# First modulation of a diffusion backbone: another order of loads and pieces, and twelve filler products behind each quarter of the second tile

## What is computed

```python
mod = jax.nn.silu(c) @ w_mod[l] + b_mod[l]                 # c for latents, c_ctx for context tokens
shift, scale, gate = jnp.split(mod, 3, axis=-1)
xn = rmsnorm(x, norm_w) * (1.0 + scale[:, None, :]) + shift[:, None, :]
proj = xn @ w_in
aq, ak, av, ag, ch, cb, cc, cg, gq, gk, gv, gg, glr = jnp.split(proj, SPLIT_POINTS, axis=-1)
...
x = x + gate[:, None, :] * mix
```

## Time and profile before

| | |
|---|---|
| median of 3 runs | 2151.84 us (2149.92 to 2151.88) |
| profiled execution | 2152.64 us, span 2150.8 us, granted clock 0.997 |
| TensorE busy | 2106.6 us, 98% of the span |
| VectorE busy | 1442.9 us, 67% |
| ScalarE busy | 647.9 us, 30% |
| first modulation | about 24 us (first quarter) to 128 us (last flip) |

### The profile page before, as it was taken

One profiled execution on the slowest core, in us unless ns is written; L12 is line 12 of the kernel. 1 busy time (PEld: TensorE's weight loads), 2 busy tenths in 40 slices (PEclk: granted clock), 3 DMA queues, 4 the chain that ended last, 5 costly groups with the idle time before them and its releaser, 6 DMA issues.

```text
span 2150.8 us, 35018 instructions
## 1 busy us (share of the span) xinstructions
PE 2106.6 (98%) x13815; PEld 1895.5 (88%) x13815; DVE 1442.9 (67%) x2797; ACT 647.9 (30%) x1092; POOL 194.0 (9%) x125
## 2 busy tenths in 40 slices
PE   5999999999999999999999999999999999999998
PEld 3778887887999999999998888888899999999998
DVE  5869888999665656766366355466666566676644
ACT  4232221321333334442134212232133333343302
POOL 0000000000000000523221000000000000043331
PEclk9999999999999999999999999999999999999999
DMA  9989786774333324564435546445343233366443
GB/s 351 376 293 320 230 282 230 234 245 160 117 105 101 99 77 135 187 210 144 121 120 162 170 149 203 132 139 150 120 129 104 75 97 105 90 209 208 152 123 141
DMA packets 357333, 365.42 MB, mean 170 GB/s; under 512 B 17670, under 2 KB 264156, under 8 KB 356572
## 3 DMA queue, kind: packets, MB, share of 16 engines
q1 hardware_dynamic: 328528, 320.67, 46.6%
q10 hardware_dynamic: 28684, 43.09, 5.3%
HBM read 304.98 MB, written 58.72 MB: 169 GB/s over the span
## 4 chain that ended last, share of the span: by engine, by line
PE 70%; DVE 2%; issue 1%; ACT 1%; DMA 1%; SPq 0%; ACTq 0%; DVEq 0%
PE psP L921 20%; PE psP L865 16%; PE psP L942 10%; PE psO L1148 6%; PE psT L875 4%; PE psT L1148 3%; PE psO L1121 3%; PE psP L1076 3%; PE psT L1087 2%; PE psP L1160 0%; PE psP L1238 0%; DVE xf L2025 0%; PE psP L1246 0%; PE psP L834 0%; DMA old<-x_scratch 0%
## 5 line engine op out<-in xcount | busy, mean ns | idle before, releaser
L1831 DVE SCALAR_TENSOR_TENSOR macc<-mraw,cond,macc 128x384 f32<-128x384 f32 (+1 forms) x960 | 389.2, 477 | 0.0
L865 PE MATMUL psP<-x_high,high 128*128 128x512 f32 x864 | 342.3, 396 | 0.6 <-DVE x_low L1887 0.6
L865 PE MATMUL psP<-x_high,low 128*128 128x512 f32 x864 | 336.6, 390 | 0.0
L865 PE MATMUL psP<-x_low,high 128*128 128x512 f32 x864 | 336.4, 389 | 0.0
L1336 ACT ACTIVATE high<-raw 128x1024 fp32r<-128x1024 f32 x128 | 135.4, 1059 | 594.3 <-PE psT L875 493.3
L921 PE MATMUL psP<-x_high,high 128*128 128x320 f32 x1024 | 242.6, 318 | 0.0
L921 PE MATMUL psP<-x_high,low 128*128 128x320 f32 x1024 | 233.4, 309 | 0.0
L921 PE MATMUL psP<-x_low,high 128*128 128x320 f32 x1024 | 232.9, 309 | 0.0
L1849 DVE TENSOR_TENSOR low<-raw,high 128x1024 fp32r<-128x1024 f32 x128 | 163.3, 1277 | 64.8 <-ACT high L1336 64.7
L865 PEld LDWEIGHTS psP<-x_high,high 128*128 128x128 f32 x864 | 162.1, 188 | 41.6 <-issue 7.7
L865 PEld LDWEIGHTS psP<-x_high,low 128*128 128x128 f32 x864 | 162.2, 188 | 34.5
(11 more groups left out here) (327 smaller groups left out, 3715.5 us busy)
## 6 DMA issues: line engine op xcount, KB each, us to landing
raw<-in_w_in_dram SPq DMA_DIRECT2D x132, 512.0 KB, 6.0
wmod<-in_w_mod_dram SPq DMA_DIRECT2D x32, 1024.0 KB, 8.2
mraw<-in_w_mod_dram SPq DMA_DIRECT2D x64, 512.0 KB, 4.5
mraw<-in_w_mod_dram SPq DMA_DIRECT2D x32, 1024.0 KB, 7.3
raw<-in_w_in_dram SPq DMA_DIRECT2D x32, 1024.0 KB, 5.7
raw<-in_w_out_dram SPq DMA_DIRECT2D x64, 512.0 KB, 4.2
old<-x_scratch SPq DMA_DIRECT2D x64, 320.0 KB, 3.2
xf<-proj_scratch SPq DMA_DIRECT2D x48, 320.0 KB, 3.6
```

Of the source, the lines that this page charges most:

```text
L865: mm = pe.matmul(latent_ps[m], own, moved, start=(k == 0 and w is whole and x is x_high), stop=(k == KT - 1 and w is rest))
L1831: m = dve.scalar_tensor_tensor(acc[:, v, 0:width], mraw[hf][:, k, 0:width], c, acc[:, v, 0:width], ALU.mult, ALU.add)
```

## The change

It moves work within the first modulation and adds fillers. Loads: tile 1's quarters go out ahead of chunk 0; in later blocks chunk 2j goes out behind quarters 0 and 1 of the odd tile instead of ahead of it. TensorE: tile 0's quarters stand behind columns 3, 6, 8 and 11 of the input instead of 3, 7, 11 and 15; tile 1's quarters stand behind the wait for the whole of x, each followed by `keep_busy(12)` on the bank `psP[0]`; two pieces of block 0 come ahead of tile 2, and 0, 1, 1, 1 and 1, 2, 1, 2 behind the quarters of tiles 2 and 3. ScalarE: block 0 casts chunk 1 in the middle of its columns. VectorE: the low part of chunk 2j stands behind the modulation's sums instead of ahead of the early sums.

```diff
+FIRST_QUARTERS = (3, 6, 8, 11)
+PIECES_LEAD, PIECES_FIRST = 2, [0, 1, 1, 1, 1, 2, 1, 2]
...
-            for t in range(MOD_CHUNKS):
-                mod_block(t)
-                front_chunk(0, t)
-                if t % 2 == 1:
-                    extra_tiles(t // 2)
+            for j in range(BLOCKS):
+                mod_block(2 * j, range(4))
+                if j == 0:
+                    mod_block(2 * j + 1, range(4))
+                    front_chunk(0, BLOCK_C * j)
+                else:
+                    mod_block(2 * j + 1, range(SUMMED_Q))
+                    front_chunk(0, BLOCK_C * j)
+                    mod_block(2 * j + 1, range(SUMMED_Q, 4))
+                front_chunk(0, BLOCK_C * j + 1)
+                extra_tiles(j)
...
-                if k % 4 == 3:
-                    mod_quarter(0, k // 4)
+                if k in FIRST_QUARTERS:
+                    mod_quarter(0, FIRST_QUARTERS.index(k))
...
-            for q in range(4):
-                mod_quarter(1, q)
...
-            def keep_busy(count):
+            def keep_busy(count, bank=psT):
 
                 for _ in range(count):
-                    pe.matmul(psT[:, 0:P], ident[:], ident[:], start=True, stop=True)
+                    pe.matmul(bank[:, 0:P], ident[:], ident[:], start=True, stop=True)
...
                     pe.wait_ge(s["x_taken"], KT)
+                    for q in range(4):
+                        mod_quarter(1, q)
+                        keep_busy(12, psP[0])
                     piece = 0
+                    for _ in range(PIECES_LEAD):
+                        block_piece(piece)
+                        piece += 1
                     for t in range(2, MOD_CHUNKS):
                         for q in range(4):
                             mod_quarter(t, q)
-                            for _ in range(PIECES_AFTER[t % 2 * 4 + q]):
+                            for _ in range((PIECES_FIRST if t < 4 else PIECES_AFTER)[t % 2 * 4 + q]):
                                 block_piece(piece)
                                 piece += 1
...
-                        for n in (2 * j, 2 * j + 1):
-                            cast_chunk(n)
+                        cast_chunk(BLOCK_C * j)
+                        if j > 0:
+                            cast_chunk(BLOCK_C * j + 1)
                         act.wait_ge(s["mod_ready"], j + 1)
                         for k in range(j * BLOCK_K, (j + 1) * BLOCK_K):
+                            if k == BLOCK_K // 2:
+                                cast_chunk(BLOCK_C * j + 1)
...
                         if j > 0:
                             flip(2 * j)
-                        chunk_low(BLOCK_C * j)
-                        if j > 0:
                             early_sums(2 * j + 1)
                         flip(2 * j + 1)
...
                                 2 * j + 2, j * BLOCK_K, BLOCK_K)
+                        chunk_low(BLOCK_C * j)
                         for k in range(j * BLOCK_K, (j + 1) * BLOCK_K):
```

More of the change, by code:

```diff
@@ L97 @@
 PIECES_AFTER, PIECES_LAST = [0, 2, 1, 2, 1, 2, 1, 2], 3
+FIRST_QUARTERS = (3, 6, 8, 11)
+PIECES_LEAD, PIECES_FIRST = 2, [0, 1, 1, 1, 1, 2, 1, 2]
 assert sum(PIECES_AFTER) + PIECES_LAST == BLOCK_PIECES and len(PIECES_AFTER) == 8
+assert PIECES_LEAD + sum(PIECES_FIRST) + PIECES_LAST == BLOCK_PIECES and len(PIECES_FIRST) == 8
 EXTRA_SLOT = RING - 1
@@ L477, in _, with mod_block @@
             wm = io["w_mod"][0].rearrange("(k p) n -> p k n", p=P)
-            def mod_block(t):
-                for q in range(4):
+            def mod_block(t, quarters):
+                for q in quarters:
                     sp.wait_ge(s[f"wmod_used{q}"], t + SEED)
```

## The result

The changed kernel takes 2156.37 us (median of 9 runs, 2155.14 to 2157.92), the kernel before 2151.88 us in the same measurement (9 runs, 2149.92 to 2154.03). The ratio is 1.002, with a 95% interval of 1.0011 to 1.0029: 4.5 us more, where 3.2 were forecast. The profiled execution took 2157.92 us, with a span of 2156.1 us.

What follows compares the result with a forecast made beforehand. TensorE bounds the kernel, so the first modulation's end shifts everything behind it. Flip 1 +7.6, flip 2 +6.9, flip 3 +5.4, then 1.1 us gained twice: +3.2 us, 2155.0 us (range 2151.3 to 2158.8).

Steps and rivals of the forecast that it cites:

- Part 1: Earlier tile 0 quarters, new load order: tile 1 starts 0.6 us later, at 40.1, and waits for no load.
- Part 2: Fillers behind tile 1's quarters: 2.68 us a group, three on the path, flip 1 7.6 us late; clock worth 0.5.
- Part 3: Two pieces ahead of tile 2: fill former load time, give back 0.7 us; flip 2 at 66.6, 6.9 us late.
- Part 4: Early sums ahead of the low part, blocks 1 to 3: gains 1.1 us each, 1.5 in block 1; loads in time.
- rival (a): Loads of odd tiles' third and fourth quarters become the bound, slower: 2157.2 to 2159.8 us; chance 0.18.
- The sum: Flip 7 comes 3.2 us later, TensorE has no gap behind it: 2155.0 us against the median, 0.15% more.
- (b): Loads in tiles 1 and 2 cover the fillers, only the gains are left: -3.7 us, 2148.1; chance 0.06.
- (c): Part 4 brings nothing, but another engine behind 128 us absorbs the delay: about 2151.8 us; chance 0.09.

Runs made afterwards that it cites:

- the loads back: Chunk 2j's load again behind all four quarters of the odd tile, on the changed kernel without fillers (0.9977), with the last group only (0.9991), with all fillers (1.0026).
- six fillers: Changed kernel with 6 instead of 12 fillers behind each quarter of tile 1: 2153.74 us, ratio 1.0001.
- the fillers alone: Kernel before plus only 12 fillers behind each quarter of tile 1, behind the wait for the whole of x: 2158.58 us, ratio 1.0027.

## Why the prediction was right, and where it wasn't

**Part 1.** Right in what matters: the loads of tile 1 cover nothing, as no quarter of it waited for one. The start was wrong by 0.6 us: the fourth stall is there, but the first one was 0.86 us instead of 1.45, and so tile 1 starts at 39.48 as before. I had taken the stalls of before as fixed.

**Part 2.** Right in mechanism and nearly in size: a group took 2.87 us instead of 2.68 (40.47 to 43.34), so three groups 0.6 us more. By luck this error made up for that of the start: flip 1 came at 52.19, forecast 52.2. The fillers' worth was put at 0.5 us, from the two slow quarters. It is 1.5 us in this order, as the pieces now stand where the clock is low (the kernel without fillers shows it). The row about the quarters was the wrong one to price it: I should have asked what runs there after the change. The sign is not touched.

**Part 3.** Right: the first piece's second half at 56.93 (57.15 forecast), tile 2 at 59.19 (59.4), flip 2 at 66.33 (66.6).

**Part 4.** Right for VectorE's order, which was also shown by itself: the even-to-odd stretch is 11.18 us in blocks 2 and 3, 1.14 us less, and flip 3 came 11.19 us behind flip 2. In block 1 the load of tile 3's third quarter, forecast to land at 72.0 and be read at 72.2, landed at 73.3. The step that failed is the time from issue to landing: I took the loads one behind the other at full rate. The four quarters' loads that were issued between 58 and 70 us took 8.0 us in the median (9.1 us in the second trace), against 5.4 and 6.9 us in the earlier trace rows. In the first trace this hid behind the early sums. In the second the load came 1.1 us later still, and the clock fell with it. That is rival (a)'s place, in block 1 only, and with another price than the one I gave: 1.1 us of load and 1.5 us of low clock, together 2.6 us from flip 2 to flip 3. In blocks 2 and 3 no trace has such a wait.

**The sum.** Flip 7 was forecast 3.2 us later and came 2.7 us later in one trace and 4.9 in the other (4.4 against the second trace of before). The measured 4.5 us, with its interval of 2.4 to 6.2 us, holds the forecast. That it lies so near is in part luck, as behind 500 us single executions moved by 1 to 3 us, which the sum had at nothing. Rivals (b) and (c) are out: without the fillers the kernel is 9.7 us quicker by the ratios, and the shift of flip 7 isn't absorbed in the projection. That the rest moves along with flip 7, as TensorE has no gap behind it, held until 500 us. Behind that I had overlooked stretches of small products in which the clock can fall (1.4 to 1.5 us between the layers, or nothing) and drifts of about a us in either direction.

**The two halves.** By flip 7, the new order without fillers gives 3.7 us and the fillers take 6.4 (8.7 by the second trace of the changed kernel). By the ratios, it is 5.4 us (0.25%) and 9.7 us (0.45%). The fillers were the whole loss, and without them the change is a gain: 0.9975 (0.9964 to 0.9986).

**What stays open.** Whether a kernel's own timing decides how often the clock falls between the layers. All four traces with the loads back have the fall, two of the ten others have it, and the three kernels of those four differ in their fillers; no run tested why. The kernel with one group and the loads back has the earliest flip 7 and falls there in both its traces, with a further 2.3 and 3.0 us lost behind 1400 us; by its ratio it gains 1.9 us, where flip 7 says 6.4. The one with all fillers and the loads back is also worse by its ratio than by its flips. It also stays open why one group behind the last quarter costs 3.1 us in the medians. One or two traces of each kernel can't settle these.

## What to carry over

Ahead of a filler stands the question who waits for the next instruction on that engine. Fillers between the quarters of a critical tile cost their full time three times, less what the clock that they hold gives back (8.6 against 1.5 us here). The same products behind its last quarter cost nothing that the flips show, but the medians of both kernels that have them are 3.1 us higher, for a reason that is not known; so judge a filler by many executions and not by one trace. A filler that does hold the clock may only bring the engine earlier to the next late load, where the clock falls instead, as it did in one trace here; look at that wait before you count the gain. Moving 1.1 us of VectorE's work out of a chain in which TensorE waits for it, into a place where VectorE waits itself, was worth that amount in each round.

## What the runs showed of the hardware

TensorE's clock fell behind waits of 2.50 and 2.64 us in block 1 and not behind waits of 1.40 and 1.92 us. The wait's length alone doesn't decide it: with six fillers the clock fell behind a wait of 2.09 us ahead of the first piece, and with the fillers alone it stayed at 1.00 behind one of 2.15 us in block 1. Behind the fall, windows of 2 us read 0.50 to 0.61 for some 4 to 6 us, and where it fell at the first pieces, two pieces of six products took 4.9 instead of 3.4 us.

Between the layers, the same instructions with the same 23 `keep_busy` products ran at 1.00 in one execution of the changed kernel and in part at 0.50 in the other, at a cost of 1.5 us; over all kernels the fall stands in 6 of 14 traces, at 1.4 to 1.5 us each. The ten records of one group took 1.38 us in the kernel before and 2.35 us in the changed one.
